# Four edits to a two-layer encoder kernel: the order of the first loads, the place of a small transpose, one weight rounding and the final store

## The chip, the cores and the metric

The kernel runs on one core of a Trainium2 chip. The metric is the device time of one execution in microseconds (us); several executions are timed, and one more is recorded by the hardware profiler. The engines are named as in the profile: PE (TensorE, matrix products; PEld is its weight load), DVE (VectorE), ACT (ScalarE), POOL (GpSimd) and SP (SyncE). PEq, ACTq, SPq and POOLq are their sequencers, which issue DMAs and wait on semaphores.

## The reference

Two layers of a hybrid encoder over 512 tokens of width 1024, in f32. What matters here:

```
for i in range(2):
    proj = x @ w_in[i]                 # GLU, gates, z, xBC and dt columns
    dt   = softplus(proj[dt columns] + dt_bias)      # 2 x 32 heads
    y_a  = conformer branch(GLU part)
    y_b  = bidirectional Mamba-2 scan(z, xBC, dt, A)
    h    = LayerNorm(alpha * x + (sigmoid(gate_a) * y_a + sigmoid(gate_b) * y_b) @ w_o)
    h2   = LayerNorm(alpha * h + SwiGLU(h))          # the "second norm"
    x    = h2 + RMSNorm(p[i] @ w_ple) * sigmoid(h2 @ w_ple_gate)
```

## The kernel before

**Layout.** Activations lie transposed, features on partitions: x is eight tiles of 128 x 512 (`KT` = 8). Every product keeps f32 accuracy by splitting: a value is rounded to a high part and its remainder is a low part, and each product is three matmuls (high x high, high weights x low activation, low weights x high activation; `three`, lines 749 to 751). A dense tile (`dense`) is 8 k-steps of three 128 x 512 matmuls, 24 in all, into one PSUM bank.

**Weights.** They stream from HBM in tiles of 512 KB, four to a cycle (`SLOTS` = 4, slots 0 to 3). For each tile SP loads it into one of two buffers `raw[:, s % 2]` (`tile`, line 299; it first waits until ACT has finished rounding the tile two places earlier). ACT's `hi` (lines 433 to 436) waits for that load and for PE to have used the slot's former tile, then writes the high part into `whi` and its negative into `wlo`. POOL's `lo` (line 328) waits for `hi` and then issues a DMA that adds the full weights from HBM onto `wlo`, which leaves the low part there. PE waits for that DMA (`slot_ready`). All instruction orders are written out by hand, one list per engine.

**Start of the kernel.** SP loads the dt weights (256 KB, line 301), x in four transfers of 512 KB (line 303), then weight tiles 0 and 1 (lines 304 and 305). ACT rounds the dt weights and the eight x tiles (line 593), then calls `hi` for tiles 0 and 1 (line 594). DVE forms the low parts of x (line 1246).

**Start of a layer.** PE computes the dt product (24 matmuls of 64 columns of weights, line 992). ACT loads its exponential table (`want(4, ACT.Exp)`), copies the result from PSUM to `sg` (line 602), rounds weight tile 2 behind the parameter load, and so on. PE waits for that copy and transposes it in four pieces (line 997). DVE then computes softplus and the decay rates in a series of small steps (lines 1312 to 1340, with ACT's Abs and Exp between), and signals `ad_ready`. PE meanwhile does dense tiles 0, 1 and 2 of the first pair of groups, waits for `ad_ready`, forms cumulative sums (`cumulative`, lines 911 and 912), does dense tile 3 and goes on to the z tiles. POOL clears `zb` once per layer (line 391) between its low-part DMAs of the first cycle and of the next.

**Second norm.** The last dense tiles before it (cycles `C_DOWN2` and `C_DOWN2 + 1`) end on PE. DVE adds them to `zb` (line 1512) and sums them (line 1258), PE forms the mean, DVE subtracts it (line 1267), ACT squares each tile (line 497) into two alternating buffers, PE averages the squares (line 888), ACT takes the square root (line 504), DVE the reciprocal (line 1272), and DVE and ACT write the normalised tiles for the next product, the gate of the last stage (cycle `C_PLE`). In its list ACT rounds all four weight tiles of `C_PLE` ahead of the squares, and loads the square-root table (line 501) right behind them.

**End.** The new x is written to `zb` tile by tile (line 1534, which signals `xn_ready`). When all eight are there, SP stores 2 MB in one DMA (line 315) and waits for it.

Of the kernel before, what the change touches and what calls it, by code (L numbers as in the profile page):

```python
# [38 lines left out]
P = 128  # L39
KT = D // P  # L40
CH = T // P
# [57 lines left out]
def build(nc, x_in, p_in, w_stream, w_dt, w_ple, par_in, out):  # L99
    ctx = ExitStack()  # L100
    with ctx:
# [177 lines left out]
        def seen(n):  # L279

            return n + EARLY
# [12 lines left out]
        @block.sync  # L294
        def _(sp):
            def tile(cyc, s):

                sp.wait_ge(hi_done[(s + 2) % SLOTS], seen(cyc + (1 if s >= 2 else 0)))
                sp.dma_start(raw[:, s % 2, :], w_stream[cyc, s]).then_inc(raw_ready[s], 16)

            sp.dma_start(tmf, w_dt[0]).then_inc(dtw_loaded, 16)
            for m in range(0, KT, 2):
                sp.dma_start(zb[:, m:m + 2, :], x_in[:, m:m + 2, :]).then_inc(x_loaded[m // 2], 16)
            sp.dma_start(raw[:, 0, :], w_stream[0, 0]).then_inc(raw_ready[0], 16)
            sp.dma_start(raw[:, 1, :], w_stream[0, 1]).then_inc(raw_ready[1], 16)
            tile(0, 2)
            tile(0, 3)
            with sp.Fori(1, ALL_CYCLES) as cyc:
                for s in range(SLOTS):
                    tile(cyc, s)  # L310
            tile(ALL_CYCLES, 0)
            tile(ALL_CYCLES, 1)

            sp.wait_ge(xn_ready, seen((LAYERS + 1) * KT))
            sp.dma_start(out, zb[:, :, :]).then_inc(out_stored, 16)
            sp.wait_ge(out_stored, 16)


        @block.gpsimd
# [104 lines left out]
        def _(act):  # L424
# [5 lines left out]
            def hi(cyc, *slots):  # L430

                for s in slots:
                    act.wait_ge(raw_ready[s], (cyc[0] + 1) * 16)
                    act.wait_ge(used[s], seen(cyc[1]))
                    act.activation(whi[:, s, :], raw[:, s % 2, :], ACT.Copy)  # L435
                    act.activation(wlo[:, s, :], raw[:, s % 2, :], ACT.Copy, scale=-1.0).then_inc(hi_done[s], 1)  # L436
# [153 lines left out]
            for m in range(KT):  # L590
                if m % 2 == 0:
                    act.wait_ge(x_loaded[m // 2], 16)
                act.activation(xh[:, m, :], zb[:, m, :], ACT.Copy).then_inc(xh_done, 1)
            hi((0, 0), 0, 1)
            settle(act)
            with act.Fori(0, LAYERS) as L:
                base = (L * CYCLES, L * BANK_CYCLES)
# [107 lines left out]
                act.dma_start(tmf, w_dt[L + 1]).then_inc(dtw_loaded, 16)  # L705
                for m in range(KT):
                    act.activation(esq[:, m, :], ge[:, m, :], ACT.Square).then_inc(esq_ready, 1)
                with act.Fori(C_DOWN2, C_PLE) as c:
                    hi(on(post, c + 1), 0, 1, 2, 3)
                k = NORMS * L + LN_2  # L710
                want(1, ACT.Sqrt)
                norm_stats(k, zb, sq_used, 2 * KT * L + KT)
                act.wait_ge(sq_used, seen(2 * KT * (L + 1)))
                norm_std()
                for m in range(KT):
                    norm_round(k, m, zb, aah, O_LN2)
                act.wait_ge(esq_used, seen(L + 1))
# [25 lines left out]
        def _(pe):  # L743
# [147 lines left out]
            def phase(base, first, end, mh, ml, nk=KT, ready=None):  # L891
# [10 lines left out]
                with pe.Fori(first, end) as c:  # L902
                    for s in range(SLOTS):
                        dense(on(base, c), s, mh, ml, nk)

            def cumulative(L):

                pe.wait_ge(ad_ready, seen(L + 1))
                a = stepf[:, ADT, :].rearrange("p (d e) -> p d e", d=2)
                for o, d, m in ((0, BWD, SU), (1, FWD, SL), (2, BWD, LW), (3, FWD, U)):  # L910
                    pe.matmul(quarters(bank[5])[:, o, :], m[:, :], a[:, d, :], start=True, stop=True)
                pe.matmul(bank[6][:, 0:GW], ones[:, :], stepf[:, ADT, :], start=True, stop=True).then_inc(cum_done, 1)

            def pair(L, base, j, first=False):

                c0 = (base[0] + j * PAIR_CYCLES, base[1] + j * PAIR_BANKS)
                G0 = L * GROUPS + j * 2
                G1 = G0 + 1
                low, high = range(KT // 2), range(KT // 2, KT)
                dense(c0, 0, xh, xl)  # L920
                dense(c0, 1, xh, xl)
                dense(c0, 2, xh, xl)
                if first:
                    cumulative(L)
                dense(c0, 3, xh, xl)
                z_tiles(on(c0, 1), 0)

                dense(on(c0, 1), 2, xh, xl)
                xs_transpose(G0)
                exponent(G0, 0, True)  # L930
                dense(on(c0, 1), 3, xh, xl)
                b_transpose(G0)
                c_dot_b(G0)
                exponent(G0, 1)
                dense(on(c0, 2), 0, xh, xl)
                exponent(G0, 2)
                state(G0, 0)
                dense(on(c0, 2), 1, xh, xl)
                exponent(G0, 3)
                state(G0, 1)  # L940
                state(G0, 2)
                z_tiles(on(c0, 2), 2, (0, 1))
                y_chunk(G0, 0)
                z_tiles(on(c0, 2), 2, (2,))
                y_chunk(G0, 1)
                y_chunk(G0, 2)
                z_tiles(on(c0, 2), 2, (3,))
                y_chunk(G0, 3)

                dense(on(c0, 3), 0, xh, xl)  # L950
                exponent(G1, 0)
                xs_transpose(G1)
                dense(on(c0, 3), 1, xh, xl, ks=low)
                y_transpose(G0, 1)
                dense(on(c0, 3), 1, xh, xl, ks=high)
                b_transpose(G1)
                c_dot_b(G1)
                exponent(G1, 1)
                dense(on(c0, 3), 2, xh, xl, ks=low)
                state(G1, 0)  # L960
                state(G1, 1)
                exponent(G1, 2)
                dense(on(c0, 3), 2, xh, xl, ks=high)
                state(G1, 2)
                exponent(G1, 3)
                dense(on(c0, 3), 3, xh, xl, ks=low)
                y_chunk(G1, 0)
                y_chunk(G1, 1)
                dense(on(c0, 3), 3, xh, xl, ks=high)
                y_chunk(G1, 2)  # L970
                y_chunk(G1, 3)

                out = on(c0, 4)
                for m in (0, 1, 3):
                    projection(out, m, ks=(0, 1))
                y_transpose(G1)
                projection(out, 2, ks=(0, 1))
                pe.wait_ge(yl_done, seen(2 * (G0 + 2)))
                for m in range(KT):
                    projection(out, m, ks=(2, 3) if m < SLOTS else range(4))  # L980
# [4 lines left out]
            with pe.Fori(0, LAYERS) as L:  # L985
# [3 lines left out]
                for k in range(KT):  # L989
                    pe.wait_ge(xl_done, seen(NORMS * KT * L + k + 1))  # L990
                    w = slice(k * 2 * HEADS, (k + 1) * 2 * HEADS)
                    q = three(bank[4][0:2 * HEADS, :], dwh[:, w], dwl[:, w], xh[:, k, :], xl[:, k, :], k == 0, k == KT - 1)
                q.then_inc(dt_done, 1)
                pe.wait_ge(dt_evac, seen(L + 1))
                settle(pe)
                for c in range(CH):
                    q = pe.transpose(bank[6][:, c * 2 * HEADS:(c + 1) * 2 * HEADS], sg[0:2 * HEADS, c * P:(c + 1) * P],
                                     ident[0:2 * HEADS, 0:2 * HEADS])
                q.then_inc(dt_done, 1)
                for j in range(PAIRS):  # L1000
                    pair(L, base, j, j == 0)
# [629 lines left out]
```

## Time and profile before

| | us |
|---|---|
| median of 3 runs | 2547.09 |
| lowest and highest run | 2543.57 and 2547.77 |
| the profiled execution's own time | 2544.5 |
| its span, first to last instruction | 2541.8 |

The span holds all that the trace shows; the 2.7 us between it and the time of the same execution lie outside of it. Mean granted clock of TensorE over the span: 0.992 of 2.4 GHz.

### The profile page before, as it was taken

How to read it: one execution, taken by the hardware profiler on the slowest of the kernel's cores; microseconds unless marked ns; L12 is line 12 of the kernel's file. 1: busy time of each engine (PE TensorE's matmuls, PEld its weight loads, DVE VectorE, ACT ScalarE, POOL GpSimd, SP SyncE). 2: the span in 40 equal slices, each digit the busy share in tenths (PEclk: the TensorE clock that was granted, in tenths of full speed). 3: DMA queues.
4: the chain of work that ended last, by engine and by line, in shares of the span. 5: the costliest groups of instructions: out<-in, count | busy, mean ns of one | idle time of the engine just before them, and what ended most of it. 6: DMA issues, size and time to landing. Idle time of an engine off the chain costs nothing.

```text
span 2541.8 us, 34936 instructions
## 1 busy us (share of the span) xinstructions
PE 2438.0 (96%) x11436; PEld 1963.9 (77%) x11436; DVE 1518.4 (60%) x2563; ACT 1316.0 (52%) x1738; POOL 631.5 (25%) x733
## 2 busy tenths in 40 slices
PE   7999999999999999999899999999999999999997
PEld 6878787787877688887577787878877767888875
DVE  5789899998743311112659998989996442111126
ACT  5645555456464654344555455554645646444454
POOL 2424324143111011111124143432421111111110
PEclk9999999999999999999999999999999999999999
DMA  7567474755789588889564755746567876888893
GB/s 192 129 138 165 100 173 100 166 124 123 175 192 222 117 189 192 192 194 206 131 159 103 168 122 127 180 101 157 123 148 172 189 189 149 193 194 187 196 209 99
DMA packets 110700, 405.69 MB, mean 160 GB/s; under 512 B 12288, under 2 KB 12288, under 8 KB 110208
## 3 DMA queue, kind: packets, MB, share of 16 engines
q0 software_dynamic: 54144, 197.16, 46.0%
q1 hardware_dynamic: 55296, 202.66, 24.0%
q10 hardware_dynamic: 1152, 4.37, 0.5%
q8 instruction: 76, 1.25, 0.2%
q14 instruction: 32, 0.26, 0.0%
HBM read 402.04 MB, written 2.10 MB: 159 GB/s over the span
## 4 chain that ended last, share of the span: by engine, by line
PE 65%; DVE 17%; ACT 8%; issue 7%; DMA 2%; POOL 1%; ACTq 0%; DVEq 0%; SPq 0%; POOLq 0%
PE bank L749 19%; PE bank L751 19%; PE bank L750 19%; DVE tmp_m L1195 4%; DVE tmp_m L1191 2%; ACT w_lo L436 2%; DVE xs_b_c L1113 2%; ACT w_hi L435 1%; DMA w_raw<-w_stream 1%; PE bank L791 1%; PE bank L792 1%; PE bank L888 1%; PE bank L794 1%; DVE y_tok L1222 1%; DMA w_lo<-w_stream 1%
## 5 line engine op out<-in xcount | busy, mean ns | idle before, releaser
L328 POOL DMA_DIRECT2D w_lo<-w_stream x376 | 327.7, 878 | 1588.1 <-ACT w_lo L436 1523.9
L749 PE MATMUL bank<-x_hi,w_hi 128*128 128x512 f32 x1728 | 687.4, 398 | 8.4 <-DMA w_lo<-w_stream 8.4
L751 PE MATMUL bank<-x_hi,w_lo 128*128 128x512 f32 x1728 | 676.3, 391 | 0.0
L750 PE MATMUL bank<-x_lo,w_hi 128*128 128x512 f32 x1728 | 676.1, 391 | 0.0
L435 ACT ACTIVATE w_hi<-w_raw 128x1024 fp32r<-128x1024 f32 x378 | 398.1, 1053 | 299.8 <-PE bank L751 241.1
L436 ACT ACTIVATE w_lo<-w_raw 128x1024 fp32r<-128x1024 f32 x378 | 395.6, 1047 | 0.0
L749 PEld LDWEIGHTS bank<-x_hi,w_hi 128*128 128x128 f32 x1728 | 326.6, 189 | 80.9 <-issue 12.7
L750 PEld LDWEIGHTS bank<-x_lo,w_hi 128*128 128x128 f32 x1728 | 326.5, 189 | 71.1 <-issue 3.3
L751 PEld LDWEIGHTS bank<-x_hi,w_lo 128*128 128x128 f32 x1728 | 326.0, 189 | 69.4
L1113 DVE SCALAR_TENSOR_TENSOR z_a<-glu_out,conv_a_params,z_a 128x497 f32 (+14 forms) x480 | 320.1, 737 | 0.0
L1479 DVE TENSOR_TENSOR glu_out<-bank,sigmoids 128x512 f32<-128x512 f32 x44 | 30.4, 692 | 414.1 <-PE bank L751 414.1
L338 POOL TENSOR_SCALAR_AFFINE_SELECT seg_rhs<-group_steps_split 128x512 fp32r<-128x512 f32 x256 | 226.0, 946 | 152.3 <-PE bank L836 127.6
L749 PE MATMUL bank<-act_a_hi,w_hi 128*128 128x512 f32 x480 | 191.3, 399 | 11.1 <-issue 7.1
L1113 DVE SCALAR_TENSOR_TENSOR xs_b_c<-conv_in,group_params,xs_b_c 128x510 f32<-128x510 f32 (+1 forms) x256 | 198.9, 844 | 0.0
L751 PE MATMUL bank<-act_a_hi,w_lo 128*128 128x512 f32 x480 | 191.9, 400 | 0.0
L750 PE MATMUL bank<-act_a_lo,w_hi 128*128 128x512 f32 x480 | 190.2, 396 | 0.0
L791 PE MATMUL bank<-w_hi,x_hi 128*128 128x256 f32 x512 | 152.9, 299 | 0.1
L792 PE MATMUL bank<-w_lo,x_hi 128*128 128x256 f32 x512 | 144.8, 283 | 0.0
L794 PE MATMUL bank<-w_hi,x_lo 128*128 128x256 f32 x496 | 140.3, 283 | 0.0
L441 ACT ACTIVATE sigmoids<-bank 128x512 f32<-128x512 f32 x92 | 55.0, 598 | 159.6 <-PE bank L751 142.3
L749 PEld LDWEIGHTS bank<-act_a_hi,w_hi 128*128 128x128 f32 x480 | 90.6, 189 | 40.0 <-issue 10.4
L441 ACT ACTIVATE conv_in<-bank 128x512 f32<-128x512 f32 x64 | 38.3, 598 | 148.9 <-PE bank L751 148.9
(213 smaller groups left out, 3720.4 us busy)
## 6 DMA issues: line engine op xcount, KB each, us to landing
w_raw<-w_stream SPq DMA_DIRECT2D x378, 512.0 KB, 4.8
w_lo<-w_stream POOLq DMA_DIRECT2D x376, 512.0 KB, 7.4
z_b<-x_in SPq DMA_DIRECT2D x4, 512.0 KB, 6.3
w_ple_in<-w_ple ACTq DMA_DIRECT2D x2, 1024.0 KB, 11.1
out<-z_b SPq DMA_DIRECT2D x1, 2048.0 KB, 6.3
ple_p<-p_in ACTq DMA_DIRECT2D x2, 512.0 KB, 6.2
params<-par_in ACTq DMA_DIRECT2D x2, 340.0 KB, 3.1
tmp_m<-w_dt ACTq DMA_DIRECT2D x2, 256.0 KB, 5.2
```

The costliest lines, as they stand in the source:

```text
L328: gp.dma_start(wlo[:, s, :], w_stream[cyc, s].bitcast(F32R), accum_op=ALU.add).then_inc(lo_done[s], 16)
L338: i = gp.affine_select(out=rhs[:, d, part], in_=ad, compare_op=ALU.is_ge, fill=0.0, base=0, pattern=[[0, HG], [sign, P]], channel_multipli ...
L435: act.activation(whi[:, s, :], raw[:, s % 2, :], ACT.Copy)
L436: act.activation(wlo[:, s, :], raw[:, s % 2, :], ACT.Copy, scale=-1.0).then_inc(hi_done[s], 1)
L749: pe.matmul(dst, wh, mh, start=first, stop=False)
L750: pe.matmul(dst, wh, ml, start=False, stop=False)
L751: return pe.matmul(dst, wl, mh, start=False, stop=last)
L791: pe.matmul(dst, xh[:, k, t], h, start=k == 0, stop=False)
L792: pe.matmul(dst, xh[:, k, t], l, start=False, stop=False)
L794: pe.matmul(dst, xl[:, k, t], h, start=False, stop=end)
L1113: q = dve.scalar_tensor_tensor(out=outs[i][:, a:b], in0=ins[i][:, a + o:b + o], scalar=w[:, k:k + 1], in1=outs[i][:, a:b], op0=ALU.mult, o ...
L1195: step(dve.scalar_tensor_tensor(out=tm[:, h, :], in0=cb[:, FWD, c, :], scalar=g[:, DTK, FWD, c, h:h + 1], in1=tm[:, h, :], op0=ALU.mult, o ...
```

## The change

- **Start.** SP issues the load of weight tile 0 behind the first of the four x transfers, no longer behind the last, and ACT calls `hi` for tile 0 after x tile 1, no longer after x tile 7. Tile 1 stays where it was.
- **Step transposes.** PE no longer waits and transposes right behind the dt product. A new function does it between the lower and the upper four k-steps of dense tile 0, in both layers.
- **Last weights.** ACT rounds slot 3 of cycle `C_PLE` behind the square root of the second norm, no longer ahead of the squares. The loop over two cycles is written out for that.
- **Store.** The result goes out in four DMAs of 512 KB, each behind its two tiles.

```
@@ sync
             for m in range(0, KT, 2):
                 sp.dma_start(zb[:, m:m + 2, :], x_in[:, m:m + 2, :]).then_inc(x_loaded[m // 2], 16)
-            sp.dma_start(raw[:, 0, :], w_stream[0, 0]).then_inc(raw_ready[0], 16)
+                if m == 0:
+                    sp.dma_start(raw[:, 0, :], w_stream[0, 0]).then_inc(raw_ready[0], 16)
             sp.dma_start(raw[:, 1, :], w_stream[0, 1]).then_inc(raw_ready[1], 16)
...
-            sp.wait_ge(xn_ready, seen((LAYERS + 1) * KT))
-            sp.dma_start(out, zb[:, :, :]).then_inc(out_stored, 16)
-            sp.wait_ge(out_stored, 16)
+            for m in range(0, KT, 2):
+                sp.wait_ge(xn_ready, seen(LAYERS * KT + m + 2))
+                sp.dma_start(out[:, m:m + 2, :], zb[:, m:m + 2, :]).then_inc(out_stored, 16)
+            sp.wait_ge(out_stored, 16 * (KT // 2))
@@ scalar
                 act.activation(xh[:, m, :], zb[:, m, :], ACT.Copy).then_inc(xh_done, 1)
-            hi((0, 0), 0, 1)
+                if m == 1:
+                    hi((0, 0), 0)
+            hi((0, 0), 1)
...
-                with act.Fori(C_DOWN2, C_PLE) as c:
-                    hi(on(post, c + 1), 0, 1, 2, 3)
+                for c in range(C_DOWN2 + 1, C_PLE + 1):
+                    hi(on(post, c), *range(SLOTS if c < C_PLE else SLOTS - 1))
                 k = NORMS * L + LN_2
                 want(1, ACT.Sqrt)
                 norm_stats(k, zb, sq_used, 2 * KT * L + KT)
                 act.wait_ge(sq_used, seen(2 * KT * (L + 1)))
                 norm_std()
+                hi(on(post, C_PLE), SLOTS - 1)
@@ tensor
+            def steps_transpose(L):
+                pe.wait_ge(dt_evac, seen(L + 1))
+                settle(pe)
+                for c in range(CH):
+                    q = pe.transpose(bank[6][:, c * 2 * HEADS:(c + 1) * 2 * HEADS], sg[0:2 * HEADS, c * P:(c + 1) * P],
+                                     ident[0:2 * HEADS, 0:2 * HEADS])
+                q.then_inc(dt_done, 1)
...
-                dense(c0, 0, xh, xl)
+                if first:
+                    dense(c0, 0, xh, xl, ks=low)
+                    steps_transpose(L)
+                    dense(c0, 0, xh, xl, ks=high)
+                else:
+                    dense(c0, 0, xh, xl)
...
                 q.then_inc(dt_done, 1)
-                pe.wait_ge(dt_evac, seen(L + 1))
-                settle(pe)
-                for c in range(CH):
-                    q = pe.transpose(bank[6][:, c * 2 * HEADS:(c + 1) * 2 * HEADS], sg[0:2 * HEADS, c * P:(c + 1) * P],
-                                     ident[0:2 * HEADS, 0:2 * HEADS])
-                q.then_inc(dt_done, 1)
```

## Rows read from the trace of the kernel before

**Rows 1.** The page, section 1 and costliest groups (line, count, busy us, mean ns).
```profile
PE 2438.0 (96%) x11436; PEld 1963.9 (77%) x11436; DVE 1518.4 (60%) x2563; ACT 1316.0 (52%) x1738; POOL 631.5 (25%) x733
...
L435 ACT ACTIVATE w_hi<-w_raw 128x1024 fp32r<-128x1024 f32 x378 | 398.1, 1053 | 299.8 <-PE bank L751 241.1
```

**Rows 2.** Chain that ended last, 0 to 60 us (start, us, what).
```profile
3.26 8.47 DMA w_raw<-w_stream
...
12.73 1.05 ACT w_lo L436
...
14.61 8.07 DMA w_lo<-w_stream
...
28.30 0.43 PE bank L749
...
29.08 0.23 PE bank L751
```

**Rows 3.** Windows view: busy time, granted clock, DMA share, GB/s.
```profile
22.80:25.90 3.10, 3.08 (x7) 2.49 (x8) 2.86 (x8) 2.00 (x2) 0.30 (x1) 0.50 1.04 252
```

**Rows 4.** Timeline of the kernel's start (start, us, engine, line, operation, [idle before, releaser]).
```profile
7.74 2.43 ACT L593 ACTIVATE x_hi<-z_b 128x512 fp32r<-128x512 f32 x4 [1.06 <-DMA z_b<-x_in]
...
8.40 3.97 DVE L1246 TENSOR_TENSOR x_lo<-z_b,x_hi 128x512 fp32r<-128x512 f32 x6 [0.92 <-ACT x_hi L593]
...
14.50 0.39 PE L751 MATMUL bank<-x_hi,w_dt_lo 128*64 128x512 f32 x1
...
17.80 0.43 PE L997 MATMUL bank<-ident,sigmoids 64*128 64x64 f32 x4 [2.92 <-ACT sigmoids L602]
...
30.62 0.43 DVE L1340 TENSOR_TENSOR steps<-steps,neg_a 128x256 f32<-128x256 f32 x1
```

**Rows 5.** Issues of POOL's queue at 16.4, 20.6 and 1288.6 us, us to landing.
```profile
w_lo<-w_stream POOLq DMA_DIRECT2D x1, 512.0 KB, 9.8
...
w_lo<-w_stream POOLq DMA_DIRECT2D x1, 512.0 KB, 8.9
...
w_lo<-w_stream POOLq DMA_DIRECT2D x1, 512.0 KB, 7.6
```

**Rows 6.** Timeline of the second layer's start.
```profile
1285.16 0.43 PE L997 MATMUL bank<-ident,sigmoids 64*128 64x64 f32 x4 [1.84 <-ACT sigmoids L602]
...
1285.88 1.06 ACT L435 ACTIVATE w_hi<-w_raw 128x1024 fp32r<-128x1024 f32 x1
...
1300.27 0.43 DVE L1340 TENSOR_TENSOR steps<-steps,neg_a 128x256 f32<-128x256 f32 x1
```

**Rows 7.** Timeline of the second norm, first layer (1210 on), second layer (2468 on).
```profile
1210.75 3.68 DVE L1267 TENSOR_TENSOR z_b<-z_b,bank 128x512 f32<-128x512 f32 x6 [1.22 <-PE bank L883]
...
1210.96 1.06 ACT L435 ACTIVATE w_hi<-w_raw 128x1024 fp32r<-128x1024 f32 x1 [3.60 <-DMA w_raw<-w_stream]
...
1212.99 1.28 ACT L501 ACT_TABLE_LOAD   x1
...
1214.39 1.13 ACT L497 ACTIVATE glu_out<-z_b 128x512 f32<-128x512 f32 x2
...
2468.37 4.87 DVE L1267 TENSOR_TENSOR z_b<-z_b,bank 128x512 f32<-128x512 f32 x8 [1.22 <-PE bank L883]
...
2469.55 1.13 ACT L497 ACTIVATE glu_out<-z_b 128x512 f32<-128x512 f32 x2
...
2482.67 2.05 ACT L509 ACTIVATE act_a_hi<-z_b,params 128x512 fp32r<-128x512 f32 x3 [4.21 <-DVE z_b L1278]
```

**Rows 8.** SP's queue at the end; landings of the store and of a load at 1269 us.
```profile
2513.09 0.34 SPq L299 DMA_DIRECT2D w_raw<-w_stream  x1
...
2535.10 0.34 SPq L315 DMA_DIRECT2D out<-z_b  x1
...
out<-z_b SPq DMA_DIRECT2D x1, 2048.0 KB, 6.3
...
w_raw<-w_stream SPq DMA_DIRECT2D x1, 512.0 KB, 3.3
```

## The prediction

> **What bounds the kernel now.** I read the page first. PE is busy for 96% of the span [rows 1], so nothing that speeds up another engine in the body can show; only places where PE stands still, or work behind its last matmul, can be won. The change touches four such places, and I read each in its own stretch.
>
> At the start the chain of waits shows what PE waits for: the load of weight tile 0, queued at 3.26 us behind the dt weights and all of x and landed at 11.7; ACT's rounding, ended at 13.8; POOL's low-part DMA, issued at 14.6 and landed at 22.7 [rows 2]. The dt product had ended at 14.9 [rows 4]. So PE stood idle from 14.9 to 22.7 but for four transposes of 0.43 us. The idle time had a second price: the granted clock was 0.50 in the stretch that follows [rows 3], the lower level of 1.2 GHz, and the matmuls came every 0.43 us until 28.9 and every 0.23 us after that [rows 2]. Fourteen of dense tile 0's 24 matmuls ran so. Tile 0 ended at 28.9 + 10 x 0.228 = 31.2, tile 1 (24 x 0.228 = 5.5) at 36.7, and there tile 2 began.
>
> At the second layer's start PE waited 1.84 us for ACT's copy, then transposed [rows 6]. In the second norm PE's products of the squares wait for ACT, which in the first layer was still waiting for a load (3.60 us) and then rounding, while DVE had begun to subtract the mean at 1210.75 [rows 7]. At the end there is one store of 2 MB, 6.3 us from issue to landing, with nothing beside it [rows 8].
>
> **Weight tile 0 earlier.** The x transfer that is now second landed at 7.7 (ACT's wait for it ends at 7.74) [rows 4]; tile 0 takes its place in SP's queue and its landing. A rounding is two passes of 1.05 us [rows 1, 2], so `hi` ends near 9.8, against 13.8. POOL issued 0.8 us behind that before (13.8 to 14.6) [rows 2], so the low-part DMA goes out at 10.6. It landed 8.1 us after issue before, with other loads in flight [rows 2]; there are others now too (the rest of x, tiles 1 and 2), so I keep 8.1: tile 0 is ready at 18.7.
>
> The price is paid by x. Everything behind tile 0 in the queue comes one transfer later (8.47 us for dt, four x transfers and tile 0 together makes some 1.5 each, an estimate), and ACT rounds x tiles 2 to 7 (0.61 us each) from 9.8 on, ending near 13.4; their low parts follow on DVE at 0.66 us each from about 10.4 [rows 4]. PE's dt product stalls after the second x tile and resumes at 11.1. If its clock rises after as much work as tile 0 did at the lower level (22.8 to 28.9) [rows 2, 3], it does 14 of its remaining 18 matmuls at 0.43 and ends near 18.1, against 14.9. This is hidden: tile 0's weights land at 18.7 anyway. Without that cover each microsecond would delay tile 0.
>
> So PE goes from the dt product to tile 0 with a gap of some 0.6 us in place of 7.9, and the first tile should run at 2.4 GHz: 5.5 us and the transposes' 0.43, ending at 24.6, against 31.2. Next come the low parts of tiles 1 and 2. Tile 1's load now shares the engines with tile 0's low-part DMA and I put it at 14.2 (estimate); rounded at 16.3, issued at 17.1. Before, that DMA took 9.8 us [rows 5], because the one ahead of it had only just been issued; now that one is nearly done, and I take 7.6, the quieter of the rows [rows 5]: 24.7. With 9.8 it would be 26.9, PE would wait 2.3. Tile 2's rounding stands behind ACT's copy of the dt product in ACT's list (18.1, 0.6 for the copy, some 0.3 for the small exponential: 19.0), ends at 21.1, is issued at 21.8, and with 8.9 [rows 5] is ready at 30.7. PE reaches it at 24.7 + 5.5 = 30.2. So tile 2 starts at 30.7, against 36.7: **6.0 us** won. The bounds: 3.0 if tile 0 runs at the lower clock and tile 1 and 2 land late, 7.0 if the landings take 7.6 throughout.
>
> **The transposes moved, first layer.** They now stand 12 matmuls into tile 0, near 21.5 to 22, and DVE's step series starts there. It took from 18.2 to 31.05 before, 12.8 us, part of it waiting for ACT and for POOL's clearing of `zb` [rows 4]. Then `ad_ready` comes near 34.8; PE wants it after tile 2, at 36.2. This wait is hidden with 1.4 us to spare; the bound is a loss of a few microseconds if POOL's clearing stretches DVE's steps. Their 0.43 us on PE stays.
>
> **The transposes moved, second layer.** PE starts tile 0 at 1283.3 and does not wait; the 1.84 us seem won. But what is late next is tile 2's low part: ACT rounds it from 1285.88, behind the parameter load, which is not moved; it is issued at 1288.6 and lands after 7.6 us, at 1296.2 [rows 5, 6]. Before, PE reached tile 2 at 1285.6 + 2 x 5.5 = 1296.6. Now it would be there at 1294.7 and waits until 1296.2. I take **0.3 us**; the upper bound is 1.8. `ad_ready` at 1300.7 [rows 6] is early enough for the end of tile 2 at 1301.7.
>
> **Slot 3 rounded behind the root.** In the first layer the squares start at 1214.39, straight behind load, rounding and table load (1210.96, 1212.99, 1.28 us). Without slot 3 ACT has its table by 1209 (slot 2 was rounded before the 3.60 us wait) and the first square waits for DVE's first tile, 1210.75 + 0.7 = 1211.5 [rows 7]: **2.9 us**. In the second layer slot 3's load was there in time, and only 2469.55 against 2468.37 + 0.7 is won, **0.45 us** [rows 7]. All of it lies on PE's path, as the chain of square, root, reciprocal and normalise follows at its own pace. The moved rounding (2.1 us) goes into ACT's idle 4.21 us under DVE's reciprocal [rows 7]; without that cover it would cost 2.1. What it issues comes some 10 us later: POOL's low-part DMA, needed only after three more dense tiles (over 16 us), and SP's next load of that buffer, needed later still. POOL and SP have nothing else to do there. I count nothing for these.
>
> **The store in parts.** SP's last weight load is issued at 2513.1 [rows 8], so the first three parts go out under PE's last tiles. Of the last one, issued at 2535.1, no row of before shows a 512 KB store; a 512 KB load took 3.3 us, the whole store 6.3 [rows 8]. Bounds: nothing won, 6.3, if the time is all latency; 3.8 won if only the bytes beyond some 1.2 us counted. I take the load's 3.3: **3.0 us**. The Trainium skill, "DMA: Bandwidth & Descriptors", section Bandwidth, speaks against this edit: it asks for at least 1 MiB per DMA, below which efficiency falls. By its rule the four parts together cost more than the whole; the trace shows that this would matter only if they stood behind the last tile, and three don't.
>
> **Sum.** 6.0 + 0.3 + 2.9 + 0.45 + 3.0 = 12.65 us. From the profiled execution's 2544.5 that is 2531.9; the median of the runs lies 2.6 above that execution, so the sum gives 2534.4 from there. I predict 2533, -0.5%. About 0.2% (5 us) is what a measurement of this kernel can tell from no change.
>
> **The rivals.**
> - *Transfers pace the start.* Tile 0 starts early, but the low parts of tiles 1 and 2 land 9.8 and 8.9 after later issues and the first tiles wait or run at the lower clock: 3.0 in place of 6.0, and the first layer's norm wins little because its late load is one execution's accident (0.45 in place of 2.9). Gain 7.2, 2539. For it: DMA share full in this stretch [rows 3]. Against: only one of the tiles is late before. Chance 0.22.
> - *No gain at the start.* The late x tiles and the wait for `ad_ready` eat all of it, and the norm wins 0.9 in all: 0.3 + 0.9 + 3.0 = 4.2, 2542. For it: ACT, DVE and PE are all shifted there. Against: PE's own idle time is 7.4 us. Chance 0.08.
> - *The stores line up behind the last tile.* If SP were held in its list until 2535, four parts at 3.3 would take 13.2 against 6.3: a loss of 6.9 for a gain of 3.0, total gain 2.75, 2543. Against: SP is free from 2513. Chance 0.02. This is the case in which the Trainium skill's rule on DMA size would bite.
> - *Slower: the clock stays down.* If PE's gaps at the start keep it at 1.2 GHz, each dense tile costs 24 x 0.2 = 4.8 us more. The gain of 12.65 is used up after 2.6 such tiles beyond those that ran so before; with four tiles and two z tiles (10 us more in all, estimated alike) it would be 29 - 2.8 - 12.65 = 14 slower, 2560. Against: the clock rose within 6.1 us of steady work. Chance 0.03.
>
> **How the numbers follow.** The forecast has 0.65: 2528 to 2537. Its upper end of gains is 7.0 + 1.8 + 2.9 + 1 + 3.8 = 16.5, 2528 to 2530. Down to 2527 and up to 2541 the range takes in the first rival and the spread of the runs, and leaves out some 0.15. Faster by over 0.2%: 0.65 and nearly all of 0.22, 0.84. Within 0.2%: 0.12. Slower: 0.04.
>
> **What would show it.** In the profile after: the first low-part DMA issued near 10.6 and dense tile 0 starting near 18.7 with 0.23 us between matmuls; tile 2 near 30.7; no wait at the cumulative sums. In the second layer PE waiting about 1.5 us for a low-part DMA ahead of tile 2. In both norms the first square right behind DVE's first subtraction, ACT rounding under the reciprocal. The last store landing 3.3 us after issue. The prediction is wrong if tile 0 starts later than 21 us or at the lower clock, if PE waits at the cumulative sums, or if the last part takes over 5 us.

## The result, and the profile after

Six runs of the changed kernel: median 2530.77 us (2527.69 to 2535.45), beside 2547.43 us for six of the kernel before: ratio 0.9937 (0.9924 to 0.995), 16.7 us faster. Repeated later (e12 below), the ratio was 0.9939 (0.9924 to 0.9954). The forecast was 2533 us. The profiled execution took 2528.91 us, with a span of 2527.3; before it was 2544.5 and 2541.8. So 14.5 of its 15.6 us lie inside the span, where the rows can show them.

The page of the changed kernel, its first line and PE's share, to set beside [rows 1]:

```profile
span 2527.3 us, 34929 instructions
...
PE 2437.7 (96%) x11436; PEld 1963.3 (78%) x11436; DVE 1520.1 (60%) x2563; ACT 1316.2 (52%) x1738; POOL 632.6 (25%) x733
```

PE does the same work in the same busy time (2438.0 before). What was won is time in which PE stood still or ran at the lower clock, and time of the store behind PE's last product.

The chain that ended last, at the start (start us, us, what), answers to [rows 2]:

```profile
1.85 6.00 DMA w_raw<-w_stream
7.88 1.06 ACT w_hi L437
...
10.43 0.70 DVE x_lo L1259
...
16.98 0.42 PE bank L755
17.41 0.23 PE bank L756
...
18.32 0.23 PE bank L754
```

The chain no longer leads from the load through the rounding and POOL's DMA to tile 0. From 10.43 on it goes through the low parts of x and PE's dt product. The matmuls change from 0.43 to 0.23 us apart at 17.4, before tile 0 begins.

The timeline of the same stretch (start, us, engine, line, operation, [idle before, releaser]), beside [rows 4]; first the two rows of the kernel before that the marks below rest on (start of dense tile 0, cumulative sums):

```profile
22.82 0.79 PE L749 MATMUL bank<-x_hi,w_hi 128*128 128x512 f32 x1 [4.58 <-DMA w_lo<-w_stream]
...
42.10 0.38 PE L911 MATMUL bank<-steps,tri_lt 128*128 128x128 f32 x2
```

and then the changed kernel:

```profile
11.18 0.69 PE L754 MATMUL bank<-x_hi,w_dt_hi 128*64 128x512 f32 x1 [1.50 <-DVE x_lo L1259]
...
18.16 0.39 PE L754 MATMUL bank<-x_hi,w_hi 128*128 128x512 f32 x1
...
20.99 0.46 PE L916 MATMUL bank<-ident,sigmoids 64*128 64x64 f32 x4
...
35.12 0.38 PE L925 MATMUL bank<-steps,tri_lt 128*128 128x128 f32 x2
```

The third x tile comes late and PE waits 1.50 us for it, which is the price that the prediction named. Tile 0 starts at 18.16, 4.66 us earlier than before, with no wait in front of it: the dt product ended there. The transposes and the cumulative sums (L925) follow without a wait; the sums came at 42.10 before and come at 35.12 now. DVE's step series, which they need, ended at 34.85, so this wait was avoided by 0.27 us, not by the 1.4 of the forecast. The landings of the low parts in POOL's queue, first one row that holds for both tile 0 (issued at 10.7 us) and tile 1 (16.0), then that of tile 2 (21.7), beside [rows 5]:

```profile
w_lo<-w_stream POOLq DMA_DIRECT2D x1, 512.0 KB, 6.9
...
w_lo<-w_stream POOLq DMA_DIRECT2D x1, 512.0 KB, 7.1
```

All three landed faster than any row that the forecast took (8.1, 7.6 and 8.9). The windows view with PE alone (busy time, granted clock, DMA share, GB/s), beside [rows 3]:

```profile
18.30:22.80 4.50, 4.50 (x23) 1.00 0.81 168
...
133.30:136.70 3.40, 3.40 (x10) 0.50 0.69 131
```

Tile 0 runs at 2.4 GHz. The second row, far into the body, is the lower level again; it returns below. Ahead of the first clock record the column reads 1.00 although the matmuls are 0.43 us apart, so at the start the distance between matmuls is the better witness.

The second layer's start, beside [rows 6]:

```profile
1275.18 0.46 PE L916 MATMUL bank<-ident,sigmoids 64*128 64x64 f32 x4
...
1284.66 0.50 PE L754 MATMUL bank<-x_hi,w_hi 128*128 128x512 f32 x1 [0.63 <-DMA w_lo<-w_stream]
```

No wait for ACT's copy, and then a wait for tile 2's low part, as forecast, but of 0.63 us instead of 1.5. The second norm in both layers, beside [rows 7]; the first row is the root in the first layer of the kernel before:

```profile
1222.61 0.69 ACT L504 ACTIVATE rstd<-bank,eps 128x512 f32<-128x512 f32 x1 [1.22 <-PE bank L888]
...
1202.71 2.48 DVE L1280 TENSOR_TENSOR z_b<-z_b,bank 128x512 f32<-128x512 f32 x4 [1.22 <-PE bank L888]
1203.44 1.23 ACT L499 ACTIVATE glu_out<-z_b 128x512 f32<-128x512 f32 x2 [3.63 <-DVE z_b L1280]
...
1211.69 0.69 ACT L506 ACTIVATE rstd<-bank,eps 128x512 f32<-128x512 f32 x1 [1.22 <-PE bank L893]
1212.27 1.05 ACT L437 ACTIVATE w_hi<-w_raw 128x1024 fp32r<-128x1024 f32 x1
...
1216.58 2.05 ACT L511 ACTIVATE act_a_hi<-z_b,params 128x512 fp32r<-128x512 f32 x3 [2.32 <-DVE z_b L1291]
...
2457.97 1.29 DVE L1280 TENSOR_TENSOR z_b<-z_b,bank 128x512 f32<-128x512 f32 x2 [1.22 <-PE bank L888]
2458.69 0.63 ACT L499 ACTIVATE glu_out<-z_b 128x512 f32<-128x512 f32 x1 [2.94 <-DVE z_b L1280]
```

The first square now follows DVE's first subtraction by 0.72 us in both layers, against 3.64 and 1.18 us. The moved rounding at 1212.27 lies beside DVE's reciprocal, and ACT's idle time there has shrunk from 4.21 to 2.32 us. The end, SP's queue and the landing of the last part, beside [rows 8]:

```profile
2502.64 21.96 SPq L317 DMA_DIRECT2D out<-z_b  x4
...
out<-z_b SPq DMA_DIRECT2D x1, 512.0 KB, 2.6
```

The last store, issued at 2524.27, takes 2.6 us; the whole took 6.3.

How far the changed kernel is ahead of the one before, at marks that both traces have (profiled executions, us):

| mark | before | after | ahead |
|---|---|---|---|
| cumulative sums, first layer | 42.10 | 35.12 | 7.0 |
| mean subtracted in the second norm | 1210.75 | 1202.71 | 8.0 |
| root of that norm | 1222.61 | 1211.69 | 10.9 |
| cumulative sums, second layer | 1302.01 | 1290.27 | 11.7 |
| mean subtracted in the second norm | 2468.37 | 2457.97 | 10.4 |
| root of that norm | 2477.77 | 2466.94 | 10.8 |
| end | 2541.77 | 2527.28 | 14.5 |

The four places of the change show, and between them the lead drifts by about 1 us either way, in stretches that the change does not touch. That drift is as large as some of the terms, so the experiments had to ask which of these steps belong to the change and which to one execution.

### The profile page after: what moved, and what is told of

Its sections match the earlier page's. It is cut to its first block, busy times and chain, and to the rows that moved or that the text cites. A ratio compares the mean times of both kernels' runs of the same rounds, so it can differ in the third digit from the quotient of the medians.

```text
span 2527.3 us, 34929 instructions
## 1 busy us (share of the span) xinstructions
PE 2437.7 (96%) x11436; PEld 1963.3 (78%) x11436; DVE 1520.1 (60%) x2563; ACT 1316.2 (52%) x1738; POOL 632.6 (25%) x733
## 4 chain that ended last, share of the span: by engine, by line
PE 65%; DVE 17%; ACT 8%; issue 7%; DMA 2%; POOL 1%; DVEq 0%; ACTq 0%; POOLq 0%; SPq 0%
PE bank L754 19%; PE bank L756 19%; PE bank L755 19%; DVE tmp_m L1208 4%; DVE tmp_m L1204 2%; ACT w_lo L438 2%; DVE xs_b_c L1126 2%; ACT w_hi L437 2%; PE bank L796 1%; PE bank L797 1%; PE bank L799 1%; PE bank L893 1%; DMA w_raw<-w_stream 1%; DVE y_tok L1235 1%; DVE tmp_y L1233 1%
## 6 DMA issues: line engine op xcount, KB each, us to landing
w_ple_in<-w_ple ACTq DMA_DIRECT2D x2, 1024.0 KB, 10.4
```

## The experiments

The kernel before scatters by itself: 31 runs beside e1 to e4 had a median of 2545.64 us and went from 2541.37 to 2553.5. Intervals below are those of the ratio, worked into us. The stages are read from each kernel's own trace.

**One part alone (e1 to e4), on the kernel before.** The edits are the four parts of the diff, one at a time.

e1, the weights:

```
+                if m == 0:
+                    sp.dma_start(raw[:, 0, :], w_stream[0, 0])...
...
+                if m == 1:
+                    hi((0, 0), 0)
+            hi((0, 0), 1)
```

> The kernel before with one part alone: weight tile 0 loaded behind the first x transfer and rounded behind x tile 1. Theory (PE's dt product at the lower clock bounds the start, and the earlier tile is worth most of the gain): the dt product ends near 18.2 us as in the changed kernel, PE then waits some 0.8 us for ACT's copy and does the four transposes (0.43 us), dense tile 0 starts near 19.4 at 0.23 us between matmuls, and the cumulative sums come near 36.0 us, against 42.1 before: 6.1 us won there, a time near 2541. Rival (the low-part DMAs bound the start, so that moving the transposes gives nothing more): the cumulative sums come at 35.1 us as in the changed kernel. Second rival (the transfers only change places): under 3 us won, over 2544.

Measured: 2544.18, 1.5 us faster (0.8 slower to 4.3 faster). The timeline:

```profile
16.15 0.43 PE L1000 MATMUL bank<-ident,sigmoids 64*128 64x64 f32 x4 [0.81 <-ACT sigmoids L605]
...
17.52 0.50 PE L752 MATMUL bank<-x_hi,w_hi 128*128 128x512 f32 x1 [0.93 <-DMA w_lo<-w_stream]
...
35.59 0.27 PE L914 MATMUL bank<-steps,tri_lt 128*128 128x128 f32 x1
```

Half of the theory falls. In this execution the third x tile was only 0.40 us late, the dt product ended near 15.2, and tile 0 did wait for its low part. So in one execution the dt product sets the start and in another the weights do; the two ends lie within some 2 us of each other. Nor did tile 0 run at 0.23 us throughout; its windows row (PE busy, clock, DMA share, GB/s):

```profile
18.70:22.00 3.30, 3.30 (x10) 0.50 0.87 163
```

So the two short waits (0.81 and 0.93 us) had a stretch at the lower clock behind them. The cumulative sums came at 35.59, 6.5 us earlier than in the profile of before. The time shows less than the stage does.

e2, the transposes:

```
+                if first:
+                    dense(c0, 0, xh, xl, ks=low)
+                    steps_transpose(L)
+                    dense(c0, 0, xh, xl, ks=high)
```

> The kernel before with one part alone: the step transposes between the two halves of dense tile 0. Theory (they only pay where PE would otherwise stand still for ACT's copy): in the first layer PE waits for weight tile 0 until 22.8 us as before and the transposes now cost 0.4 us inside the tile, at the second layer's start PE does not wait for ACT's copy (1.84 us) but waits 0.5 to 1.5 us for tile 2's low part: +0.3 to +0.8. In sum no change, 2546.5 to 2548. Rival (the clearing of zb on POOL stretches DVE's step series, which now starts near 28.4 us and before took 12.8 us): the cumulative sums wait beyond 42.5 us, 1 to 4 us slower, 2548.5 to 2551.

Measured: 2547.65, 2.0 us slower (0.8 to 5.3). Timeline, and a windows row (busy of each engine, clock):

```profile
22.08 0.79 PE L749 MATMUL bank<-x_hi,w_hi 128*128 128x512 f32 x1 [7.15 <-DMA w_lo<-w_stream]
...
26.40 0.46 PE L911 MATMUL bank<-ident,sigmoids 64*128 64x64 f32 x4
...
1212.66 2.73 PE L888 MATMUL bank<-glu_out,ones_over_d 128*128 128x512 f32 x3 [2.23 <-ACT glu_out L497]
```

```profile
1212.90:1216.30 3.40, 3.40 (x5) 1.29 (x5) 0.73 (x2) 0.88 (x3) 0.00 (x0) 0.50 1.01 264
```

PE waits 7.15 us in one piece, with the transposes no longer inside that wait but inside a tile that runs at the lower clock. The sums came at 40.53, half a microsecond later than in the three other traces with an unaltered start (39.88 to 39.98). The rival's price shows in the sign only: the sums did not wait. The second layer's step needs several traces to show: from the root of the second norm to the cumulative sums of the second layer it is 79.36 to 81.00 us in the five traces with the transposes in their old place (median 79.42) and 78.58 to 79.26 in the seven in which they moved and tile 2's rounding did not (79.21 in e2; median 78.72), 0.7 us. The last rows belong to the norm, which this kernel has unaltered: PE waits 2.23 us for ACT's first square, and the clock is at 0.50 in the stretch behind it. A wait there can cost twice.

e3, the rounding: `hi(on(post, C_PLE), SLOTS - 1)` behind `norm_std()`, and one slot fewer ahead of the squares.

> The kernel before with one part alone: slot 3's weights rounded behind the root of the second norm. Theory (the late load in the first layer's norm is there in every execution): 2.9 us won in the first layer and 0.45 in the second, the rounding under DVE's reciprocal, a time near 2544. Rival (the late load was one execution's accident): 0.45 in each layer, 0.9 in all, near 2546.5.

Measured: 2538.88, 6.8 us faster (3.8 to 8.9), more than either theory. The squares, in the first and the second layer:

```profile
1208.15 1.23 ACT L497 ACTIVATE glu_out<-z_b 128x512 f32<-128x512 f32 x2 [3.59 <-DVE z_b L1268]
...
2466.22 1.23 ACT L497 ACTIVATE glu_out<-z_b 128x512 f32<-128x512 f32 x2 [1.01 <-DVE z_b L1268]
```

In both they follow DVE at once. What the part is worth is the time from DVE's first subtraction to ACT's root. In the five traces without this edit (before, e1, e2, e4, e9; two norms each) it was 9.4 to 13.1 us, mean 11.4; in the nine traces with it, 8.97 in all eighteen norms. So 2.4 us a norm, 4.9 in all. The late load is the rule in both layers: nine of the ten unedited norms waited 1.5 to 3.9 us for it, and the second layer of [rows 7], from which the forecast took 0.45, was the one that did not. The longest three of the ten (12.8, 12.8, 13.1) have a stretch at 0.50 in them, as in e2's row.

e4, the store in four parts.

> The kernel before with one part alone: the result stored in four parts. Theory: the last part of 512 KB lands 2.6 us after its issue, against 6.3 us for the whole, and nothing else moves: 3.7 us won, near 2543.7. Rival (the prediction's price, 3.3 us): 3.0 us, near 2544.4. Second rival (the other 1.1 us that the changed kernel's runs won over its span also come from the store, as fewer bytes are under way at the end): 4.5 us or more, under 2543.

Measured: 2542.74, 2.9 us faster (0.8 slower to 4.3 faster). The landing of the last part:

```profile
out<-z_b SPq DMA_DIRECT2D x1, 512.0 KB, 2.6
```

The store took 6.28 us in every trace that stores at once and the last of four parts 2.62 or 2.63, so 3.66 us is the step. The time outside of the span was 1.9 us here and 2.0 in the runs of before: nothing more is won there.

The four medians add to 9.1 us, against 14 to 17 for the whole. The steps by the rows add to 4.4 - 0.5 + 0.7 + 4.9 + 3.7 = 13.2 (the first two against a start at 39.98, the third the second layer's start), and in the first layer the transposes give 0.7 instead of -0.5 once the weights are early (35.59 in e1 against a median of 34.90 with both). The intervals, some 2.5 us each way for each of the four, cover the rest. Whether anything beyond that ties the parts together stays open.

**What bounds the new start (e5, e6)**, on the changed kernel. e5 loads weight tile 0 first of all and rounds it ahead of x:

```
+            sp.dma_start(raw[:, 0, :], w_stream[0, 0])...
             sp.dma_start(tmf, w_dt[0])...
```

> The changed kernel with weight tile 0 loaded ahead of the dt weights and x, and rounded ahead of x. Theory (the dt product, which runs at the lower clock until it has worked without a break for some 6 us, sets the start of dense tile 0, and the weights do not): the weights' low part lands near 15 us in place of 17.6, the dt product starts near 8.4 instead of 6.9 but has no break of 1.5 us in it, ends near 16.8, and dense tile 0 starts there, 1.3 us earlier than in the changed kernel (18.16). Rival (the weights set it): tile 0 starts near 15.5, or the later x costs what the weights win and it starts at 18 or later. In the whole time 1.3 us is not measured; the trace decides.

e6 adds work for PE ahead of it:

```
+            pe.wait_ge(consts, 4)
+            for _ in range(12):
+                pe.matmul(bank[5][:, 0:P], ones[:, :], mean1[:, :], start=True, stop=True)
```

> The same, and PE multiplies constants twelve times (results unused) from about 1.8 us until the dt product begins. Theory (the lower clock of the dt product is what costs): the dt product runs at 0.23 us between matmuls where x does not hold it up and ends near 13.5 to 14; dense tile 0 starts when its weights land, near 15, 3 us before the changed kernel's. Rival (what PE did before does not carry over, or the constants delay the dt product): 0.43 us between matmuls as before and tile 0 at 16.8 or later.

Measured: 2532.17 and 2532.40, with 2543.75 for the kernel before; ratios 0.9947 (0.993 to 0.9963) and 0.9952 (0.9935 to 0.9968), no better than the changed kernel. In e5 dense tile 0 starts at 17.61, behind the dt product as the theory has it, but 0.55 us earlier and not 1.3, since x came later still (first product at 9.28). Its matmuls drew together 6.0 us after that, at 15.3; the "some 6 us" of the theory is not the same everywhere, as in the kernel before it was 5.0 us (6.94 to 11.9). The timeline of e6:

```profile
3.41 5.34 PE L1001 MATMUL bank<-ones_over_d,ones 128*128 128x128 f32 x24 [3.41 <-POOL tri_lt L366]
9.37 0.45 PE L752 MATMUL bank<-x_hi,w_dt_hi 128*64 128x512 f32 x1 [0.62 <-DVE x_lo L1260]
...
17.27 0.49 PE L752 MATMUL bank<-x_hi,w_hi 128*128 128x512 f32 x1 [2.22 <-DMA w_lo<-w_stream]
```

and its windows row behind that:

```profile
18.90:22.20 3.30, 3.30 (x12) 2.15 (x11) 0.02 (x1) 1.33 (x2) 0.86 (x1) 0.51 0.96 179
```

After the constants the dt product runs at 0.23 us from its second matmul on and ends at 14.9, 2.7 us earlier than in e5. Then the low part of tile 0 is late (8.2 us from its issue at 8.92), PE waits 2.22 us, and the tile runs partly at 0.51. The sums come at 35.85, later than in e5 (34.56). The time won on the clock was given back as a wait, and the wait took the clock. The Trainium skill, "TensorE: Matmul & The Clock Gate", Part 1, says that the lower clock is the default state and that activity releases it; e6 agrees at the dt product, with 0.23 us between matmuls in place of 0.43.

**The head of the layers and finer stores (e7)**, on the changed kernel: `hi(base, 2)` ahead of the copy of the dt product, and eight stores of 256 KB.

> The changed kernel with two edits far apart. First, tile 2's weights are rounded at the head of each layer, ahead of ACT's copy of the dt product: by the theory that tile 2's low part is late next at the second layer's start, PE's wait of 0.63 us for it goes, and nothing else moves there; a rival is that the copy becomes late and the transposes wait. Second, the result is stored in eight parts of 256 KB: if the landing is mostly a fixed latency the last part takes 2.0 to 2.4 us in place of 2.6, if it is mostly bytes it takes 1.3 (half of 2.6); a third way is that it is no better as eight stores line up, 2.6 or more.

Measured: 2531.62; 0.995 (0.9933 to 0.9966).

```profile
34.16 0.38 PE L925 MATMUL bank<-steps,tri_lt 128*128 128x128 f32 x2
...
1275.58 0.43 PE L916 MATMUL bank<-ident,sigmoids 64*128 64x64 f32 x4 [1.00 <-ACT sigmoids L607]
...
out<-z_b SPq DMA_DIRECT2D x1, 256.0 KB, 2.0
```

The wait for tile 2 went and the rival came: the transposes wait 1.00 us for ACT's copy at the second layer. The last part takes 2.0 us, a further 0.6. Together 2048, 512 and 256 KB took 6.28, 2.62 and 2.02 us, which is 1.4 us plus the bytes at some 430 GB/s. The Trainium skill, "DMA: Bandwidth & Descriptors", Anatomy of one DMA, gives 2.0 us plus bytes at 436 GB/s, fitted on GpSimd's path; the slope agrees, and the fixed part of these stores from SP is smaller.

**What the scatter comes from (e8 to e11).** These were meant to take PE's longest waits out of the body, and all four had the edit at the wrong place, which the traces showed only afterwards. e8:

```
-                state(G0, 0)
-                dense(on(c0, 2), 1, xh, xl)
+                dense(on(c0, 2), 1, xh, xl, ks=low)
+                state(G0, 0)
+                dense(on(c0, 2), 1, xh, xl, ks=high)
```

> The changed kernel with one order on PE altered, far from the change: in every pair the first state product of the first group, for which PE waits 3.13 us, is put behind the first half of the dense tile that follows it. It tests what the scatter between executions comes from. Theory (the granted clock falls to 0.50 after PE has stood still for 2 us or more, in some executions and not in others, 1.7 us each time): the eight waits shrink to some 0.4 us, the stretches at 0.50 in the pairs (5 or 6 of 8 in the traces so far) vanish, and the time falls by 8 x 2.7 for the waits and 5 to 6 x 1.7 for the clock, 30 us, near 2500. Rival (DVE's series sets the pace of the pair, and the wait comes back at the next product): no gain or under 5 us, but if the wait comes back in pieces under 2 us, the stretches at 0.50 go all the same.

Measured: 2539.85, 0.9991 (0.9978 to 1.0003): some 8 us above e5 to e7, which were measured beside it. The waits view (total, times, longest):

```profile
PE bank L856 <- DVE x_weighted L1156: 22.0, 8, 3.1
```

In the changed kernel this row is 25.0, 8, 3.1. The wait of 3.13 us belongs to the pair's second group. The edit moved the first group's product, on which DVE's states hang, and PE now waits 1.14 to 1.41 us for these a little later, eight times, where the changed kernel waits 0.57.

e9 (kernel before) and e10 (changed kernel) put matmuls on constants ahead of the same product, and ahead of the first tile of the phase from C_UP0:

```
+                for _ in range(12):
+                    pe.matmul(bank[6][:, :], SLR[:, :], xh[:, 0, :], start=True, stop=True)
                 state(G0, 0)
...
+                    for _ in range(14):
+                        pe.matmul(bank[0][:, :], SLR[:, :], whi[:, 0, 0:4 * P], start=True, stop=True)
```

> The kernel before, and PE multiplies constants (results unused) while it waits: 12 matmuls ahead of the first state product of every pair (a wait of 3.13 us) and 14 ahead of the first tile behind the second norm (3.56 us). The waits themselves stay. Theory (the granted clock falls because PE has stood still, and which of the waits set it off in one execution is chance, so this makes most of the scatter between executions): the stretches at 0.50 inside the pairs and behind the norm vanish, 6 of 8 and 2 of 2 in the profile of before, 1.7 us each: 13 us faster than before, near 2532, and the executions lie closer together. Rival (the falls have another cause than standing still): as many stretches at 0.50, the same time as before, or slower where the constants outlast a wait.

> The changed kernel with the same matmuls on constants in PE's waits. Theory: against the run before this one it shows what the change is worth with that chance taken out. By the stages of the traces so far: 5.0 at the start, 0.2 at the second layer's start, 2.3 and 1.5 to 2.0 in the two norms, 3.65 at the store: 13 us less than that run, near 2518. Rival (the changed kernel's further gain in the first timing, 16.7 us, is real): 16 us or more less.

> The same as the run before this one, with tile 2's weights rounded at the head of each layer and the result stored in eight parts. Theory: 0.6 to 1.0 us at the start, 0.6 at the end, about 1.5 in all, too little for the time to tell; the stages of the trace show it. Rival: no gain, as the rounding of tile 2 now makes ACT's copy of the dt product late and the transposes wait (1.0 us at the second layer's start) what the tile's low part waited before.

Measured: e9 2569.89, e10 2553.13, e11 2549.86, with 2546.52 for the kernel before. The costliest groups of e9 (busy us, mean ns):

```profile
L941 PE MATMUL bank<-x_hi,tri_gt_r 128*128 128x512 f32 x96 | 23.8, 396 | 0.0
...
L896 PE MATMUL bank<-w_hi,tri_gt_r 128*128 128x512 f32 x28 | 7.7, 424 | 0.0
```

and its row of the waits, the same 25.0 us in eight waits as in the changed kernel:

```profile
PE bank L851 <- DVE x_weighted L1147: 25.0, 8, 3.1
```

The 124 matmuls at 0.228 us are 28.3 us of PE's time, 4.5 of which went into short waits of the first group (0.57 a pair in the kernel before, none in e9); 23.8 us, and the kernel is 23.4 slower. The long waits stayed where they were, behind the second group and behind the second norm, so the theory on the clock was not tried as meant. Two things can be kept. Work added to PE in the body costs its full time, as 96% busy says. And between e9 and e10 the change is worth 16.8 us on this other base, within the scatter of its other timings. e11 is 3.3 us below e10, where 1.5 were expected; twelve runs of each, which spread over 12 and 15 us, do not separate the two. One thing in these traces was not asked for: a stretch at 0.50 lies behind four, three and one of the eight waits in e9, e10 and e11, against five or six in each of the eleven other traces. That is one trace each, and the edit also shifted the times at which the waits fall, so what did it stays open.

What the traces show without an edit: in the kernel before, the granted clock is at 0.50 behind five of the eight 3.13 us waits in the pairs (not six, as the expectation of e9 has it) and behind both second norms, in the changed kernel behind six and both. From one such wait to the next it is 151.3 to 151.6 us where no such stretch lies behind the first, and 152.9 to 153.4 us where one of 3.4 us does (the ten traces with unaltered pairs). Shorter waits have one behind them too, in some executions: that for the first square in e2 and e4 (2.23 and 1.93 us), and that of the transposes at the second layer's start in e4 (2.05 us); this change takes both of those away. In e1 it was two waits of 0.81 and 0.93 us, so the 2 us in the expectation of e8 is no bound. That this makes the scatter is not shown by an edit, but the times bear it out in part. Each timed execution has its mean granted clock on record, and over the 67 of the kernel before that were timed beside the experiments the span is 1.7 us shorter for each 0.001 of it (correlation -0.71). That goes with about half of the variance; where the rest comes from stays open.

**The changed kernel again (e12).**

> The changed kernel again, unaltered, on the same chip as the three other runs. Theory (the parts add up by the stages, 12 to 13 us): 0.995 of the kernel before. Rival (the first timing's 16.7 us): 0.9935 or less.

Measured: 2532.45 beside 2546.52, 14.1 us; 0.9939 (0.9924 to 0.9954). Its start:

```profile
18.15 0.49 PE L754 MATMUL bank<-x_hi,w_hi 128*128 128x512 f32 x1 [1.38 <-DMA w_lo<-w_stream]
...
30.67 0.50 PE L754 MATMUL bank<-x_hi,w_hi 128*128 128x512 f32 x1 [0.73 <-DMA w_lo<-w_stream]
```

Here tile 0 waits for its low part (7.9 us to landing) and tile 2 for its own, at 30.67: the prediction put that one at 30.7. This is the start that was forecast; the one profiled first was the quicker kind. With the loads in this order (e1, e7, e8, e10, e11 and e12, and the first profile) tile 0 waits for its low part in four of seven traces, 0.31 to 1.38 us. No version that was run beats the changed kernel by more than the timing can tell.

## Why the prediction was right, and where not

| step | forecast | the two profiled executions | over all traces |
|---|---|---|---|
| start, first layer | 6.0 | 7.0 | 5.1 |
| second layer's start | 0.3 | 0.8 | 0.7 |
| second norm, both layers | 3.35 | 3.3 | 4.9 |
| store | 3.0 | 3.7 | 3.7 |
| sum | 12.65 | 14.8 | 14.4 |

The span shows 14.5 because the lead also drifted between the steps. The third column compares all the traces that share a stage: the sums came at 39.88, 39.98, 39.98 and 42.10 us with the old start (median 39.98), and at 34.59, 34.67, 35.12 and 36.25 with the new one (median 34.90). The second layer's start is the difference of the medians given at e2. The two timings of the change, 16.7 and 14.1 us, lie on either side of this sum, and both above the forecast's 12.65.

- **Weights earlier.** The mechanism held: tile 0 near 18.2 at 2.4 GHz, and tile 2 at 29.7 in the first profile and 30.7 in e12. The forecast had the weights as bound (18.7) and the dt product hidden at 18.1; the dt product ended at 18.16 and the weights came at 17.6, so the order of the two was wrong and the size right. The gain of 6.0 was measured from a poor start: in [rows 2] the lower clock held until 28.9 us and the sums came 2.1 us later than in the three other traces; against their median it is 5.1.
- **Transposes.** In the first layer `ad_ready` was never waited for, as forecast, though with 0.27 us to spare instead of 1.4, and alone the moved transposes lose half a microsecond, since they only pay where ACT's copy would be waited for. In the second layer the named wait for tile 2 came, but shorter (0.63 us for 1.5), so 0.3 was too little: 0.7.
- **Rounding behind the root.** The chain was as described, and its cover too. The mis-sized term is the second layer: 0.45 was taken from the one norm in ten whose load was in time. The rival "one execution's accident" had it the wrong way round; the mean is 2.8 us in the first layer and 2.1 in the second.
- **Store.** The value taken, 3.3 us, came from a load with others in flight beside it. Alone, the part took 2.6 and 3.7 were won, near the forecast's bound of 3.8: by the fit at e7 only 1.4 us do not depend on the bytes. The Trainium skill's rule on DMA size ("DMA: Bandwidth & Descriptors", Bandwidth) agrees with the trace as far as efficiency goes, 512 KB in 2.62 us against 2048 KB in 6.28. But the three earlier parts lay under PE's last tiles, so what they lost did not show; with eight parts it did not either.
- **Rivals.** Transfers pace the start in e12, where it costs some 1.1 us, not 3. The clock did not stay down. The gain at the start was not eaten up by the late x tiles or by `ad_ready`, close as the latter came. The stores did not line up.

One term was too large (start, by 0.9) and three were too small (second layer's start by 0.4, norm by 1.55, store by 0.7), so a sum that came within 2 us of the rows owes something to luck: it says less about its parts than it seems to.

## What to carry to other kernels

A gain that is read as a wait in one execution should be looked up in as many passes of the same place as the trace has, both layers here, before one value is taken: the norm's late load was in nine of ten passes and the one that lacked it set the term. At a start, give each of the two or three paths that meet its own end time, and expect a won wait to move to the path that ends next: moving the weights further forward and running PE at 2.4 GHz earlier won nothing. At the end of a kernel the bytes of the last store are exposed time, and earlier parts are free as long as PE still works.

## What was not expected of the hardware

- DVE's 128x256 `tensor_scalar` at the start took 4.17 us beside POOL's clearing of `zb` (3.85 us), for an instruction that takes 0.29 elsewhere in the same series. In the first layer of the kernel before it ran at 23.66 us, ahead of the clearing (26.13); the later transposes put it beside the clearing (25.88 and 25.95). It cost nothing, as the series still ended 0.27 us before PE came for it.
- The DMAs of the low parts of tiles 0 to 2, each 512 KB from POOL's queue, took between 6.1 and 9.8 us from issue to landing over these traces. The order of issue tells a part of that: tile 1's took 8.8 to 9.8 us in the five traces in which it went out 1.8 us behind tile 0's, and 6.8 to 7.9 in the seven in which it went out some 5 us behind, as the forecast had reckoned (7.6). What is left is 1 to 2 us for the same tile in the same order, and a start cannot be forecast closer than that from one trace.
